# Dense attention scores as three rounded products, with filler transposes at the start

## What is computed

```
qb = (rms_norm(cq, q_norm_g) @ w_uq).reshape(B, Lp, B_HEADS, B_NOPE + B_ROPE)
q_nope, q_pe = qb[..., :B_NOPE], qb[..., B_NOPE:]          # 64 and 32 rows of a head
q_pe = apply_rope(q_pe, cos[:, None, :], sin[:, None, :])
kvb = (rms_norm(ckv, kv_norm_g) @ w_ukv).reshape(B, Lp, B_HEADS, B_NOPE + B_V)
k_nope, vb = kvb[..., :B_NOPE], kvb[..., B_NOPE:]
k_pe = apply_rope(kpe, cos, sin)                           # one set of 32 rows for all heads
lb = (einsum('bqhd,bkhd->bhqk', q_nope, k_nope) + einsum('bqhr,bkr->bhqk', q_pe, k_pe)) * scale_b
lb = where(causal, lb, NEG);  pb = softmax(lb);  ob = einsum('bhqk,bkhd->bqhd', pb, vb)
```

## Time and profile before

| | us |
|---|---|
| median of 3 timed runs | 345.21 (345.17 to 345.22) |
| the profiled execution | 343.74 |
| its span, first to last instruction | 341.9 |
| PE busy in the span | 322.1 (94%) |
| DVE busy | 226.4 (66%) |
| POOL busy | 186.9 (55%) |
| ACT busy | 171.7 (50%) |
| chain that ended last, PE's share | 74% |
| the same, DVE's share | 17% |

### The profile page before, as it was taken

One profiled execution on the slowest core, in us unless ns is written; L12 is line 12 of the kernel. 1 busy time (PEld: TensorE's weight loads), 2 busy tenths in 40 slices (PEclk: granted clock), 3 DMA queues, 4 the chain that ended last, 5 costly groups with the idle time before them and its releaser, 6 DMA issues.

```text
span 341.9 us, 6103 instructions
## 1 busy us (share of the span) xinstructions
PE 322.1 (94%) x2130; PEld 271.5 (79%) x2130; DVE 226.4 (66%) x588; ACT 171.7 (50%) x378; POOL 186.9 (55%) x187
## 2 busy tenths in 40 slices
PE   0799999999999999999999999999999999999990
PEld 0488977788778888887887888797978897998990
DVE  6763120269966799988875985467677766444686
ACT  4774553354433455566434554667587753622221
POOL 4342999959322262256322578598659371650462
PEclk9999999999999999999999999999999999999997
DMA  7464343229423121201400132222333110130023
GB/s 274 174 202 161 123 126 124 92 66 291 148 69 113 47 94 61 71 20 58 133 2 15 63 117 102 71 88 92 96 93 95 63 63 0 63 125 0 3 100 146
DMA packets 11565, 32.86 MB, mean 96 GB/s; under 512 B 2392, under 2 KB 2392, under 8 KB 11536
## 3 DMA queue, kind: packets, MB, share of 16 engines
q1 hardware_dynamic: 8944, 27.08, 23.3%
q10 hardware_dynamic: 2592, 5.40, 5.4%
HBM read 29.83 MB, written 4.81 MB: 101 GB/s over the span
## 4 chain that ended last, share of the span: by engine, by line
PE 74%; DVE 17%; issue 3%; ACT 3%; DMA 2%; SPq 0%; DVEq 0%; ACTq 0%
PE ps_j L1273 42%; PE ps_o L1538 6%; PE ps_s L1483 4%; PE ps_s L1487 3%; DVE iw L1110 3%; DVE top L1106 3%; PE ps_t L1273 2%; PE ps_j L1325 2%; PE ps_t L1507 2%; PE ps_s L1454 2%; DMA res<-in_x 2%; DVE iw L1091 2%; PE ps_t L1512 2%; PE ps_j L1373 1%; DVE tmp L1063 1%
## 5 line engine op out<-in xcount | busy, mean ns | idle before, releaser
L561 POOL TENSOR_TENSOR wl<-raw,wh 128x1024 fp32r<-128x1024 f32 (+2 forms) x33 | 77.4, 2352 | 66.5 <-ACT wh L568 66.4
L1273 PE MATMUL ps_j<-hh,wh 128*128 128x512 f32 (+2 forms) x216 | 75.6, 350 | 0.1
L1273 PE MATMUL ps_j<-hl,wh 128*128 128x512 f32 (+2 forms) x216 | 74.8, 346 | 0.0
L1273 PE MATMUL ps_j<-hh,wl 128*128 128x512 f32 (+2 forms) x216 | 74.5, 345 | 0.0
L691 POOL TENSOR_SCALAR pr<-pr,rden 128x528 f32<-128x528 f32 (+1 forms) x64 | 35.2, 570 | 52.1 <-DVE rden L1152 52.1
L1273 PEld LDWEIGHTS ps_j<-hh,wh 128*128 128x128 f32 (+1 forms) x216 | 40.3, 186 | 6.5 <-issue 1.0
L1273 PEld LDWEIGHTS ps_j<-hl,wh 128*128 128x128 f32 (+1 forms) x216 | 40.3, 186 | 5.2 <-issue 0.2
L1273 PEld LDWEIGHTS ps_j<-hh,wl 128*128 128x128 f32 (+1 forms) x216 | 40.3, 187 | 5.1
L568 ACT ACTIVATE wh<-raw 128x1024 fp32r<-128x1024 f32 (+2 forms) x35 | 36.0, 1041 | 0.7 <-DMA raw<-in_weights 0.7
L703 POOL TENSOR_TENSOR bm<-bias,mask 128x144 f32<-128x144 f32 (+3 forms) x32 | 25.5, 835 | 0.0
L886 ACT ACTIVATE pr<-ps_s,mn 128x528 f32<-128x528 f32 (+3 forms) x32 | 16.9, 540 | 14.9 <-DVE mn L1138 14.9
(11 more groups left out here) (283 smaller groups left out, 816.5 us busy)
## 6 DMA issues: line engine op xcount, KB each, us to landing
raw<-in_weights SPq DMA_DIRECT2D x37, 512.0 KB, 3.7
bias_by_distance<-bias_vector ACTq DMA_DIRECT2D x1, 2624.0 KB, 12.7
bias<-bias_by_distance ACTq DMA_DIRECT2D x8, 264.0 KB, 2.9
res<-in_x SPq DMA_DIRECT2D x4, 512.0 KB, 4.9
out<-res SPq DMA_DIRECT2D x3, 512.0 KB, 2.6
pt<-in_ln_emb_g SPq DMA_DIRECT2D x1, 512.0 KB, 4.9
pt<-in_ln_emb_b SPq DMA_DIRECT2D x1, 512.0 KB, 6.5
q_b<-qpe ACTq DMA_DIRECT2D x8, 64.0 KB, 2.0
```

What stands on the lines that cost most here:

```text
L561: eng.tensor_tensor(ring_of(False, b), raw_of(b), ring_of(True, b).bitcast(F32), ALU.subtract).then_inc(done, 1)
L1273: last = pe.matmul(dst, a, b, start=n == 0 and part[0], stop=n == count - 1 and part[1])
```

## The change

- **Scores.** `q_b` and `k_b` become fp32r with a high and a low part for each head of a pair. A score tile is now three matmuls (high·high, low·high, high·low) in place of one f32 matmul.
- **Evacuations.** ACT writes the high parts of both heads (two copies for `qn`, two for each half of `kn`), and DVE, which waits for each ACT copy, subtracts it from the PSUM bank to get the low part. EMPTY, the count of evacuations per job, goes from (1, 1) to (2, 2) for both.
- **Rotary rows.** q's rotary rows are split by an ACT copy (ROPEH) and a DVE subtraction (ROPEL), stored to DRAM (ROPED, four DMAs in all) and read back from there into `q_b`. k's rotary rows are made in a tile `kpe` of their own and split into `k_b` (KROWS: two ACT copies, two DVE subtractions). POOL's copy of them goes.
- **Sums of squares.** ACT's Square writes the high part, DVE still computes the square and subtracts. The sums are taken by four fp32r matmuls each, in place of two f32 ones.
- **Fillers.** `busy(36)`, `busy(6)` and `busy(6)`: transposes of the identity into an unused bank, ahead of the first transposes.
- **Order.** The `va` jobs per dense head change from 1, 1, 2, 0, 2, 1, 2, 0 to 1, 2, 1, 1, 1, 2, 1, 0. Around PV one `kn` half goes before and one behind, and for the sparse heads of the last pair PV moves behind one output job.

```diff
-            jobs = [("va", *va.pop(0)) for _ in range((1, 1, 2, 0, 2, 1, 2, 0)[g])]
+            jobs = [("va", *va.pop(0)) for _ in range((1, 2, 1, 1, 1, 2, 1, 0)[g])]
             if g % 2 and more:
-                jobs = [("qn", p + 1)] + jobs + [("kn", p + 1, 0), ("kn", p + 1, 1)]
+                jobs = [("qn", p + 1), ("kn", p + 1, 0)] + jobs
+                jobs.insert(2 if g > 1 else 3, ("kn", p + 1, 1))
+                if g == 1:
+                    jobs[1:3] = jobs[2:0:-1]
+                    jobs[2:] = [jobs[2], jobs[4], jobs[3]]
...
         if pair is not None and not late:
+            job(*jobs.pop(0), extra=0)
             order += [("PV", pair, 0), ("PV", pair, 1)]
+            job(*jobs.pop(0), extra=0)
...
                     if kind == "cq":
                         act.activation(cq_t[:, n, :], bank, ACT.Copy).then_inc(job_act, 1)
+                        act.wait_ge(job_act, BY_ACT[j + 1])
+                        act.activation(cqh[:, n, :], cq_t[:, n, :], ACT.Square).then_inc(sq_high, 1)
...
                     elif kind == "qn":
                         if n:
                             act.wait_ge(s_mm, 4 * n)
-                        act.activation(q_b[0:HD, 0, :], bank[0:HD, :], ACT.Copy, scale=-SCALE_B).then_inc(job_act, 1)
+                        for e in range(2):
+                            act.activation(q_b[0:HD, 0, e, :], bank[HD * e:HD * e + HD, :], ACT.Copy,
+                                           scale=-SCALE_B).then_inc(job_act, 1)
...
                     elif kind == "qn":
                         if n:
                             dve.wait_ge(s_mm, 4 * n)
-                        dve.tensor_scalar(q_b[0:HD, 1, :], bank[HD:P, :], -SCALE_B, None, ALU.mult).then_inc(job_dve, 1)
+                        for e in range(2):
+                            dve.wait_ge(job_act, BY_ACT[j] + e + 1)
+                            dve.scalar_tensor_tensor(out=q_b[0:HD, 1, e, :], in0=bank[HD * e:HD * e + HD, :], scalar=-SCALE_B,
+                                                     in1=q_b[0:HD, 0, e, :].bitcast(F32), op0=ALU.mult,
+                                                     op1=ALU.subtract).then_inc(job_dve, 1)
...
+                elif stage == "ROPEL":
+                    n = arg[0]
+                    dve.wait_ge(rope_h, n + 1)
+                    s = slice(512 * n, 512 * n + 512)
+                    dve.tensor_tensor(qpe[:, s].bitcast(F32R), qpe[:, s], qpe_h[:, s], ALU.subtract).then_inc(rope_l, 1)
...
             pe.wait_ge(made, 2)
+            busy(36)
             pe.wait_ge(xn_done, 1)
...
                         for c in range(2):
-                            last = pe.matmul(ps_s[:, 0:NQ], ones[:, :], cq_sq[:, c, :], start=c == 0, stop=c == 1)
+                            for x in (cqh, cql):
+                                last = pe.matmul(ps_s[:, 0:NQ], ones[:, :], x[:, c, :], start=c == 0 and x is cqh,
+                                                 stop=c == 1 and x is cql)
...
                                 if g < HEADS:
-                                    pe.matmul(dst, q_b[:, e, i * P:(i + 1) * P], k_b[:, e, a:b], start=i >= 2,
-                                              stop=b <= NK[i] - 144, skip_group_check=True)
+                                    for n, (x, y) in enumerate(((0, 0), (1, 0), (0, 1))):
+                                        pe.matmul(dst, q_b[:, x, e, i * P:(i + 1) * P], k_b[:, y, e, a:b],
+                                                  start=i >= 2 and n == 0, stop=n == 2 and b <= NK[i] - 144,
+                                                  skip_group_check=True)
```

More of the change, by code:

```diff
@@ L168, in schedule @@
             job("qpe", 0)
+            order += [("KROWS",), ("ROPEH", 0), ("ROPEL", 0)]
         if h < 7:
@@ L177, in schedule @@
     job("qpe", 1)
-    order.append(("FLIP",))
+    order += [("FLIP",), ("ROPED", 0)]
     pick(2)
     job("gate", 6, extra=0)
+    order += [("ROPEH", 1), ("ROPEL", 1)]
     pick(4)
@@ L187, in schedule @@
     job("uv", 0, 3, extra=0)
-    order.append(("ZERO",))
+    order += [("ZERO",), ("QPE", 0)]
     job("qn", 0, extra=0)
@@ L192, in schedule @@
     job("uv", 0, 4, extra=0)
-    order.append(("QPE", 0))
+    order.append(("ROPED", 1))
     pick(3)
@@ L321, in build @@
           sin_t, out):
+    rope_dram = nc.dram_tensor("rope_rows", (HEADS, ROPE, 2, NQ), F32, kind="Internal").ap()
     vec_dram = nc.dram_tensor("bias_vector", (HEADS, VECW), F32, kind="Internal").ap()
@@ L799, in _ @@
                             act.wait_ge(s_mm, 4 * n)
-                        act.activation(k_b[0:HD, 0, 264 * m:264 * m + 264], bank[0:HD, 0:264],
-                                       ACT.Copy).then_inc(job_act, 1)
+                        for e in range(2):
+                            act.activation(k_b[0:HD, 0, e, 264 * m:264 * m + 264], bank[HD * e:HD * e + HD, 0:264],
+                                           ACT.Copy).then_inc(job_act, 1)
                     elif kind == "va":
@@ L820, in _ @@
                                                bank[HD * e:HD * e + HD, 0:264], ACT.Copy).then_inc(job_act, 1)
+                elif stage == "KROWS":
+                    act.wait_ge(kp, 4)
+                    for e in range(2):
+                        act.activation(k_b[HD:HD + ROPE, 0, e, :], k0, ACT.Copy).then_inc(kr_act, 1)
+                elif stage == "ROPEH":
+                    n = arg[0]
+                    act.wait_ge(rope_t, n + 1)
+                    s = slice(512 * n, 512 * n + 512)
+                    act.activation(qpe_h[:, s].bitcast(F32R), qpe[:, s], ACT.Copy).then_inc(rope_h, 1)
+                elif stage == "ROPED":
+                    n = arg[0]
+                    act.wait_ge(rope_h, n + 1)
+                    act.wait_ge(rope_l, n + 1)
+                    for v, x in enumerate((qpe_h, qpe)):
+                        act.dma_start(rope_dram[4 * n:4 * n + 4, :, v, :],
+                                      x[:, 512 * n:512 * n + 512]).then_inc(rope_out[n], 16)
                 elif stage == "QPE":
                     n = arg[0]
-                    act.wait_ge(rope_t, n // 2 + 1)
+                    act.wait_ge(rope_out[n // 2], 32)
+                    if n == 0:
+                        act.wait_ge(kr_act, 2)
+                        act.wait_ge(kr_dve, 2)
                     if n:
@@ L1033, in _ @@
                             dve.wait_ge(s_mm, 4 * n)
-                        dve.tensor_copy(k_b[0:HD, 1, 264 * m:264 * m + 264], bank[HD:P, 0:264]).then_inc(job_dve, 1)
+                        s = slice(264 * m, 264 * m + 264)
+                        for e in range(2):
+                            dve.wait_ge(job_act, BY_ACT[j] + e + 1)
+                            dve.tensor_tensor(k_b[0:HD, 1, e, s], bank[HD * e:HD * e + HD, 0:264],
+                                              k_b[0:HD, 0, e, s].bitcast(F32), ALU.subtract).then_inc(job_dve, 1)
                     elif kind == "ka":
@@ L1236, in _, with busy @@
         def _(pe):
+            def busy(count):
+                for _ in range(count):
+                    pe.transpose(ps_j[:, 1, 0:P], ident[:, :], ident[:, :])
             pe.wait_ge(made, 2)
+            busy(36)
             pe.wait_ge(xn_done, 1)
@@ L1248, in _ @@
                 if n:
+                    busy(6)
                     pe.wait_ge(meta_s, 1)
                 pe.matmul(vec_bank(n), rb[:, :], oh_sb[:, a:b], start=True, stop=True).then_inc(vec_mm, 1)
+            busy(6)
             pe.wait_ge(xn_done, 5)
@@ L1414, in _ @@
                         pe.wait_ge(vec_cp, 2)
-                        pe.wait_ge(squared, 2)
+                        pe.wait_ge(squared, 4)
                         for c in range(2):
-                            last = pe.matmul(ps_s[:, 0:NQ], ones[:, :], cq_sq[:, c, :], start=c == 0, stop=c == 1)
+                            for x in (cqh, cql):
+                                last = pe.matmul(ps_s[:, 0:NQ], ones[:, :], x[:, c, :], start=c == 0 and x is cqh,
+                                                 stop=c == 1 and x is cql)
                     else:
-                        pe.wait_ge(squared, 4)
+                        pe.wait_ge(squared, 8)
                         for m in range(2):
-                            last = pe.matmul(ps_s[:, 512 + 512 * m:776 + 512 * m], ones[:, :],
-                                             ckv_sq[:, 264 * m:264 * m + 264], start=True, stop=True)
+                            for x in (ckh, ckl):
+                                last = pe.matmul(ps_s[:, 512 + 512 * m:776 + 512 * m], ones[:, :],
+                                                 x[:, 264 * m:264 * m + 264], start=x is ckh, stop=x is ckl)
                     last.then_inc(ss_mm, 1)
```

72 lines of the change are left out of this document (52 added, 20 removed).

## The result

The changed kernel takes **355.75 us**, median of six runs (five from 354.3 to 357.34, and one, disturbed, of 1098, which the comparison leaves out), against 345.22 before: ratio 1.0308, interval 1.0279 to 1.0338. The forecast was 350.7, range 343.2 to 353.0. The profiled execution took 354.83 (span 353.0), 11.1 more than that of before; what follows splits these 11.1 us.

What follows compares the result with a forecast made beforehand. PE was taken as the bound, with DVE as full from 130 to 142 us. New waits 11.15, less old waits 0.6 and 0.3, scores 2.6 and front 2.2, gave +5.45: 350.7 us, range 343.2 to 353.0.

Steps and rivals of the forecast that it cites:

- PE's waits: Dense heads: PE waits for the serial chain of q's evacuations and for late DVE, 11.15 us in sum.
- ROPEL: Second ROPEL, a 128x512 DVE subtraction in its full stretch: taken as 1.5 us, bounds 0.7 and 3.0.
- Rival 3: Second ROPEL is locked out by POOL, 3.0 us in place of 1.5: 352.2 us, chance 0.12.
- The clock: PE's new waits, longest 2.7 us: clock taken to hold, being still 1.00 three us after PE's last matmul.
- rival 4: PE's clock falls to 1.2 GHz twice in the new waits, 3 us more: 353.7 us, chance 0.04.
- Scores: Dense heads: 2.25 us on PE in place of 2.57, a gain of 2.6 us over eight heads, off PE's path in full.
- Front: Before the heads: faster transposes of x gain 1.0 us and cheaper sums of squares 1.2, together 2.2.
- Behind head 8: Nothing of weight changes there: PE stays the bound, and the moved PV leaves the same jobs ahead of the last transposes.
- The 0.4: Head 7, about 2 us late, costs the first k of the sparse branch a PE wait of 0.4 us.

Runs made afterwards that it cites:

- rope_late: The changed kernel with the second ROPEL on DVE moved behind the first pair's q and k evacuations, where POOL has no work: 354.12 us, ratio to before 1.0287.
- keep_all: The changed kernel with filler transposes on PE ahead of all four waits for q's evacuation (28, 22, 24, 14): 353.84 us, ratio to before 1.0266.
- q_first: The changed kernel with ACT's high part of q ahead of the odd head's exps and DVE's low part ahead of its top-k half: 351.99 us, ratio to before 1.0202.
- both: The changed kernel with the edits of q_first and rope_late together: 348.15 us, ratio to before 1.0104.
- old_order: The changed kernel with the three edits of the job lists undone, so the va jobs stand in their old order: 351.99 us, ratio to before 1.0205.
- both_old: The changed kernel with the edits of q_first and rope_late and the old order of the jobs: 349.72 us, ratio to before 1.0136.
- bal: both_old with two top-k halves moved to where DVE idled and 16 more fillers in PE's wait for the one-hot table: 345.51 us, ratio to before 1.0024.
- keep: The changed kernel with 22 and 24 filler transposes on PE ahead of only the second and third waits for q's evacuation: 353.63 us, ratio to before 1.0254.

## Why the prediction was half right

Slower, as forecast; nearly twice as much as forecast, and above the range. Step by step, in the profiled execution:

- **PE's waits: right in place and size, but for ROPEL.** Forecast and measured: first `va` 2.1 and 3.26; scores of head 1 1.2 and 0.99; first half of k 2.5 and 2.52; PV 0.3 and 0.21; k behind head 3 2.65 and 2.74; the next `va` 0.45 and 0.32; behind head 5 1.1 and 0.45, and 1.56 and 0.32. 10.75 forecast, 11.92 measured. The difference, 1.17, is that of the first wait (1.16), which has what ROPEL took above the 1.5 that I assumed; the rest, from 0.2 too long to 0.5 too short, evens out, which is luck.
- **ROPEL: wrong, mis-sized**, 2.67 for 1.5. I had both bounds, and took the value of the nearest row, which is that of one case: POOL was 1.4 us under way there, and 0.29 here. Rival 3 was the case, at 0.12.
- **The clock: wrong, and the step that failed.** "It was still 1.00 three us after PE's last matmul; the longest new wait is 2.7." One gap, read to 337 us, told nothing of the others: in the same trace the granted clock is 0.50 from 338 us on, and in after it was 0.50 right behind the wait of 2.5 and 1.6 us behind that of 2.7. Nor does the 1.00 mean full pace everywhere: in rope_late 13 of the first fillers start in the 2.8 us up to 4.3 and 24 in the 2.6 us from 4.4, both under a recorded 1.00. keep_all shows 3.05 us, for the 3 of rival 4, to which I gave 0.04. My own rows held the warning: the transposes at 14.52 had the pace of 1.2 GHz under a recorded 1.00, where "PE had done only little, with gaps, up to 13.4". I read it for the gain in front and not for the new waits. Without the 3.05 the median would be 352.7, inside the range.
- **Rivals 3 and 4 as alternatives: wrong.** They are separate mechanisms and both came. With 1.5 and 3 more the forecast would have been 355.2.
- **Scores: over-sized.** 2.6 forecast; 8 x 0.21 = 1.7 measured, a head 2.32 for 2.53 by the starts of its first matmul and of the next job.
- **Front: 2.2 forecast, 1.8 measured here**, and not steady: the wait for the table was not seen as one in which the clock falls.
- **Behind head 8: wrong, and only the number fits.** The 0.4 was to be a wait for the first k of the sparse branch, ahead of the scores of head 8; the trace has no such wait from 200 us to these scores. The 0.5 measured is behind them, where I had said that the moved PV changes nothing; with the old order it is gone (126.6 us to the end, before 126.7).

Sum: 5.45 forecast + 1.17 waits + 3.05 clock + 0.9 scores + 0.4 front - 0.4 for the k of the sparse branch + 0.5 behind head 8 = 11.1, and measured 11.1. What each wait has for a cause is less settled than the sum: q_first and both take some of it from the chain, but none takes all. In the old place of the `va` jobs (old_order) two of the four large waits are gone, which the prediction told only in a half sentence and did not price.

## What to carry to other kernels

Moving work from a full PE to evacuations is worth only what the evacuating engines have free in that very stretch: here 1.7 us of matmul bought 12 us of waits and 3 of low clock, and the best arrangement found gave them back but for 2.4 us more than leaving the scores alone (88.67 for 86.26). A new wait on PE costs its length and, at times, the low clock behind it; price both, or give PE filler matmuls there. Rivals that rest on different mechanisms are to be added up, not only weighed against each other.

## What the runs showed of the hardware

- Waits of 1.2 to 3.3 us on PE were sometimes followed by matmuls at 1.2 GHz (granted clock 0.50), 16 of them in each of two places in after, and sometimes not. The shortest is in both_old: 1.15, and 0.36 shortly behind it, then 0.83 over 20 us; bal has the same two waits (1.17 and 0.36) and 1.00. The same wait of 3.26 at the first `va` left the clock alone in after (1.00) and took it in keep (0.81 over 9 us) and in q_first (0.83); that of 2.74 took it in after and not in rope_late. TensorE: Matmul & The Clock Gate, Part 1, of the Trainium skill tells why the place can vary: the hardware watches the activity on a beat of its own, which doesn't start with the kernel. This fits the scatter; no run here shows that beat itself.
- That makes a kernel with such waits uneven: after ran from 354.3 to 357.34, at mean clocks of 0.979 and 0.969, before from 344.91 to 346.05.
- Filler transposes into a bank that is free, 0.11 each, held the clock in every wait that they filled (six of six, in one profiled execution each of keep and keep_all; the first of these waits had left it alone in after too).
- A DVE subtraction with both inputs in SBUF took 2.67 when POOL's had started 0.29 us earlier, and 0.68 with POOL at rest. The 1.52 of before started when POOL's instruction had been under way for 1.4 us.
